# Input projections of a second block in three split products, its raw state parked in DRAM, and a last down group by token halves

## The chip, the cores and the metric

The kernel runs on one core of one Trainium2 chip. The metric is the device time of one execution in microseconds (us). Matrix products run on TensorE (PE in the profile), elementwise work on VectorE (DVE), ScalarE (ACT) and GpSimd (POOL), and SyncE (SP) issues most of the DMAs. The engines run their own instruction lists in order and wait for each other on semaphores.

## The reference, cut to what matters

Two transformer blocks follow each other on a state of 1024 tokens x 1024 features, in float32. The first has windowed attentions and a mixture of experts. Its output is `rms_norm(h, norm_final_g)`. The second block takes it as `x` and computes, in short:

```
hn   = rmsnorm(x) * attn_norm
proj = hn @ w_in_2             # q, k (256 each), v, gate (512 each), low (16), s5 u (256), rg x, rg gate (256 each)
y    = concat(gla(q, k, v, gate, low), s5(u), rg_lru(rx, rgate))
x    = x + y @ w_out_2
f    = rmsnorm(x) * mlp_norm
g, u = f @ w_up_2              # 2816 columns each
x    = x + (gelu(causal_conv(g)) * u) @ w_down_2
out  = rmsnorm(x) * final_norm
```

`gla` is a gated linear attention with four heads in chunks of 64 tokens; `s5` is a diagonal complex recurrence with 16 groups of 64 states; `rg_lru` is a gated real recurrence behind a short causal convolution.

## The kernel before

**Layout.** The state `hT` has features on partitions: eight tiles `Hp[k]` of 128 x 1024 (4096 KB in all). Work tiles are pages `Wp[i]` of the same size, and `Bp[k]` are eight of them. PSUM is used as four slots of 128 x 1024. `take()` numbers the uses of the slots in program order, and `slot(n)` waits until the use four earlier has been emptied. `mm_done` counts the products done.

**Weights.** SP loads weight units of 128 x 1024 into a ring of four places. Most products run as three: a float32 operand is split into a high part (fp32r, rounded) and the rest, and high x high, high x rest and rest x high are summed (`parts_tile`, L748 to 764: 48 matmuls of 512 columns for a 128 x 1024 output). For these GpSimd makes both parts of each weight unit (`split`, L554: a copy and a subtraction), in two buffers in turn. The 18 input units of the second block are the exception: they are used unsplit from the ring, in plain float32. `column_tile` (L708) gives 14 tiles of q, k, gate, u, rx and rgate with features on partitions; `token_tile` (L766) gives the four tiles of v with tokens on partitions, by swapping the operands. The first two columns run as `first_pair` (L718), tile by tile as the normalized state appears.

**Start of the second block.** The norm at the end of the first block and the one at the start of the second are folded: VectorE forms two rows of roots, spreads them on a diagonal (L1995), TensorE turns each into a full tile (L981), and VectorE writes `Bp[k]` (normalized input, L2001) and rescales `Hp[k]` in place (residual, L2005).

**S5 rounds.** For j = 0..8 TensorE's list is: the two state inputs of round j (L1025), one projection tile (L713), then the output product of round j-1 (L1044), which waits for GpSimd. In round 6 the low-rank product of 16 columns (L1033) stands behind the projection. VectorE multiplies the two state inputs from PSUM by a turning factor (L2078 to 2081), adds (L2083, L2084) and scans (L2085, L2086); GpSimd turns the states back with six operations on SBUF (L671 to 676) and asks for the factors two rounds ahead (L654). VR, VI and the factors have two buffers each.

**GLA.** Behind the rounds come three more value tiles, the gate products, norms, key transposes (L1073), chunk states (L1088), scores (L1098), and then the four heads: product of a head (L1123 to 1131), square on ScalarE, sum, root and scaling on VectorE, transposes (L1108). The output projection, whose first pair takes the parts that are ready first, follows.

**Feed-forward.** The 22 hidden tiles run in four groups of 6, 6, 6 and 4; behind each group the eight output tiles are updated by its product (`P_DOWN`, added into hT on L1817). With the last group VectorE also sums the squares for the final norm (L1528 after ScalarE's square, L1182). Then TensorE sums over partitions (L783), ScalarE takes roots, VectorE forms the diagonal (L1535), TensorE spreads it (L792), VectorE applies it tile by tile (L1546), and SP stores each tile.

## Time and profile before

| | us |
|---|---|
| three runs, median (lowest to highest) | 2489.38 (2489.29 to 2492.99) |
| the profiled execution, its own time | 2489.56 |
| its span in the trace | 2487.8 |
| TensorE busy | 2357.7 |
| GpSimd busy | 897.3 |
| VectorE busy | 1154.5 |
| ScalarE busy | 575.9 |

Times in the trace are counted from the start of the span. The second block starts at about 1216 us; its projections and S5 rounds run to about 1549, the four heads from 1601 to 1649. The granted clock of TensorE is given as a share of full speed: 1.00 is 2.4 GHz and 0.50 is 1.2 GHz. A float32 matmul appears as two records in the trace and overlaps its neighbours, so lengths of tiles are taken from start to start.

### The profile page before, as it was taken

To read this page: it belongs to the slowest core of one execution; us is meant where nothing else is said; L and a number is where in the kernel's file an instruction comes from. 1 tells how busy PE (TensorE), PEld (TensorE's weight loads), DVE (VectorE), ACT (ScalarE), POOL (GpSimd) and SP (SyncE) were. 2 spreads that over 40 slices of the span, in tenths; PEclk is the share of its full clock that TensorE was granted. 3 is DMA by queue.
4 is the path that set the end of the run, shared out by engine and by line. 5 is a ranking of instruction groups with operands and counts; after the bars stand their busy time and mean duration, and the time that the engine had idled before them with its cause. 6 is when DMAs were issued, how large, how long until landed. Compare 5 with 4: busy or idle time off the path is not lost.

```text
span 2487.8 us, 28689 instructions
## 1 busy us (share of the span) xinstructions
PE 2357.7 (95%) x11280; PEld 1799.0 (72%) x11280; DVE 1154.5 (46%) x1862; ACT 575.9 (23%) x809; POOL 897.3 (36%) x546
## 2 busy tenths in 40 slices
PE   7999999998999399998899999899999999999996
PEld 6888799997976266665444338778888888888885
DVE  7996444445522222222767856635432243133144
ACT  3100265676632111111121004111110011011011
POOL 2323534444423765700304861224332332332331
PEclk9999999999999799999899999779999999999998
DMA  4232122232322787822511210001111111111102
GB/s 153 77 119 85 50 67 75 67 90 69 114 94 95 285 303 298 311 102 110 190 40 45 76 59 26 9 27 50 49 40 47 60 41 45 60 49 39 58 26 76
DMA packets 76946, 228.76 MB, mean 92 GB/s; under 512 B 5456, under 2 KB 37328, under 8 KB 69904
## 3 DMA queue, kind: packets, MB, share of 16 engines
q1 hardware_dynamic: 58160, 140.60, 16.6%
q0 software_dynamic: 8576, 45.42, 5.0%
q10 hardware_dynamic: 10080, 40.90, 4.3%
q8 instruction: 94, 1.54, 0.3%
q14 instruction: 36, 0.29, 0.0%
HBM read 173.42 MB, written 53.48 MB: 91 GB/s over the span
## 4 chain that ended last, share of the span: by engine, by line
PE 91%; DVE 3%; issue 2%; ACT 1%; DMA 1%; POOL 1%; SPq 0%; DVEq 0%; POOLq 0%; ACTq 0%
PE ps L759 14%; PE ps L761 14%; PE ps L763 14%; PE ps L851 7%; PE ps L713 7%; PE ps L948 4%; PE ps L828 4%; PE ps L837 3%; PE ps L771 2%; PE ps L741 2%; PE ps L932 2%; PE ps L928 2%; PE ps L930 2%; PE ps L929 2%; PE ps L1025 1%
## 5 line engine op out<-in xcount | busy, mean ns | idle before, releaser
L759 PE MATMUL ps<-work_part 128*128 128x512 f32 x1568 | 484.0, 390 | 0.8 <-DVE work L2225 0.8
L763 PE MATMUL ps<-work_part 128*128 128x512 f32 x1568 | 482.7, 389 | 0.0
L564 POOL CAST work_part<-ring 128x1024 fp32r<-128x1024 f32 (+2 forms) x116 | 113.4, 977 | 825.1 <-PE ps L763 680.4
L761 PE MATMUL ps<-work_part 128*128 128x512 f32 x1216 | 374.4, 389 | 0.0
L759 PEld LDWEIGHTS ps<-work_part 128*128 128x128 f32 x1568 | 293.7, 188 | 62.2 <-DVE work L2225 1.3
L763 PEld LDWEIGHTS ps<-work_part 128*128 128x128 f32 x1568 | 294.4, 188 | 61.2
L568 POOL TENSOR_TENSOR work_part<-ring,work_part 128x1024 fp32r<-128x1024 f32 (+2 forms) x116 | 266.7, 2299 | 20.8 <-PE ps L1131 11.6
L761 PEld LDWEIGHTS ps<-work_part 128*128 128x128 f32 x1216 | 228.3, 188 | 47.4
L851 PE MATMUL ps<-work,hT 128*128 128x64 f32 x1600 | 195.8, 273 | 2.6 <-ACT hT L1251 2.1
L851 PEld LDWEIGHTS ps<-work,hT 128*128 128x128 f32 x1600 | 189.9, 193 | 4.6 <-ACT hT L1251 2.4
L1817 DVE TENSOR_TENSOR hT<-ps,hT 128x1024 f32<-128x1024 f32 x48 | 58.8, 1225 | 283.8 <-PE ps L763 267.3
L713 PE MATMUL ps<-work,ring 128*128 128x512 f32 x384 | 166.6, 592 | 0.0
L1768 DVE CUSTOM_DVE_ANT_0 hT<-ps,hT 128x1024 f32<-128x1024 f32 (+2 forms) x86 | 85.1, 990 | 130.1 <-PE ps L828 127.6
L713 PEld LDWEIGHTS ps<-work,ring 128*128 128x128 f32 x384 | 72.9, 190 | 91.4 <-issue 91.4
L828 PE MATMUL ps<-work_part 128*128 128x512 f32 (+1 forms) x448 | 125.5, 397 | 11.6 <-issue 8.1
L1499 ACT ACTIVATE work<-ps,cst 128x1024 f32<-128x1024 f32 x22 | 26.6, 1207 | 398.6 <-DVE ps L2220 398.6
L626 POOL TENSOR_TENSOR experts_lo<-pages,experts_hi 128x1024 fp32r<-128x1024 f32 x48 | 113.5, 2365 | 12.7 <-DMA pages<-w_moe 9.3
L948 PE MATMUL ps<-pages,work 128*128 x248 | 111.6, 592 | 1.6 <-DVE work L1949 1.6
L761 PE MATMUL ps<-hT_part,work_part 128*128 128x512 f32 x352 | 108.5, 390 | 0.0
L1242 ACT ACTIVATE hT<-hT,negm 128x1024 f32<-128x1024 f32 (+2 forms) x86 | 82.6, 961 | 97.1 <-DVE negm L1768 97.1
L1251 ACT ACTIVATE hT<-ps 128x1024 f32<-128x1024 f32 (+2 forms) x128 | 104.6, 818 | 1.4 <-PE ps L837 1.4
L2220 DVE TENSOR_TENSOR ps<-ps,cst 128x1024 f32<-128x1024 f32 x22 | 27.1, 1233 | 144.2 <-PE ps L763 137.6
(348 smaller groups left out, 3520.1 us busy)
## 6 DMA issues: line engine op xcount, KB each, us to landing
pages<-w_moe SPq DMA_DIRECT2D x16, 2048.0 KB, 9.2
ring<-w_up_units SPq DMA_DIRECT2D x44, 512.0 KB, 3.3
ring<-w_in_units SPq DMA_DIRECT2D x42, 512.0 KB, 3.5
pages<-w_moe SPq DMA_DIRECT2D x16, 1024.0 KB, 7.3
x_slots<-hT SPq DMA_DIRECT2D x31, 512.0 KB, 3.5
work<-x_slots ACTq DMA_DIRECT2D x31, 512.0 KB, 5.7
y_slots<-work ACTq DMA_DIRECT2D x31, 512.0 KB, 2.7
ring<-w_down_units SPq DMA_DIRECT2D x24, 384.0 KB, 3.0
```

Source lines behind the costliest of these rows:

```text
L564: pool.tensor_copy(WHI[n % 2][:, 0:cols], w).then_inc(whi_ready, 1)
L568: pool.tensor_tensor(WLO[n % 2][:, 0:cols], w, WHI_F[n % 2][:, 0:cols], ALU.subtract).then_inc(wlo_ready, 1)
L626: lo = pool.tensor_tensor(XLOW[:, at_lo:at_lo + S], w, hi.bitcast(f32), ALU.subtract)
L713: mm = pe.matmul(ps[:, half * HALF:(half + 1) * HALF], w[:, k * P:(k + 1) * P], rhs[k][:, half * HALF:(half + 1) * HALF], start=(k == 0), ...
L759: pe.matmul(ps[:, c], whi[:, w], hi[k][:, c], start=(k == 0), stop=False)
L761: pe.matmul(ps[:, c], whi[:, w], lo[k][:, c], start=False, stop=False)
L763: mm = pe.matmul(ps[:, c], wlo[:, w], hi[k][:, c], start=False, stop=(k == len(hi) - 1))
L828: mm = pe.matmul(ps[:, b * HALF:b * HALF + w], QS[h % 2][:, i * P:(i + 1) * P], part[h % 2][:, c0:c0 + w], start=(part is KH), stop=(part ...
L851: mm = pe.matmul(ps[:, 0:DH], PT[u % 2][:, j * P:(j + 1) * P], Wp[16 + k0 + j][:, h * DH:(h + 1) * DH], start=(j == 0), stop=(j == k1 - k0 ...
L948: mm = pe.matmul(ps[:, half * HALF:(half + 1) * HALF], HAT[b % 2][:, f * P:(f + 1) * P], xw[:, bass.ds(pages[b] + 4 * S + f * S + half * H ...
L1251: act.activation(PT[u % 2][:, 0:(k1 - k0) * P], PS[bank(n)][:, 0:(k1 - k0) * P], ACT.Copy).then_inc(pT_ready, 1)
L1768: dve.tensor_tensor_reduce(out=banks(SB[u % 3][:, 0:nk]), in0=scores, in1=banks(bias), scale=-1.0, scalar=3.0e38, op0=ALU.add, op1=ALU.min ...
```

## The change

- **Split projections.** The 18 input units of the second block run as `parts_tile`, too. The normalized input goes to three buffers `HN`; ScalarE rounds it to `HHI[k]` (in the pages of `Bp`) and VectorE writes the rest `HLO[k]` into the memory of hT. The ring's places 0 and 2 take the raw unit, ScalarE writes the high part into place 1 or 3 (`round_in2`), and GpSimd writes the rest over the raw unit (`rest_in2`), one unit ahead of each S5 round. A unit may be loaded when the product two units earlier is done.
- **Values.** The value tiles are computed with features on partitions, copied by ScalarE and turned by eight transposes (`turn_v`, `take_v`).
- **Low-rank product.** Its weights are split once by GpSimd; 48 matmuls of 512 columns take the place of 16 float32 ones.
- **State in DRAM.** Since HLO overwrites hT, SP stores hT to `h_keep` when the first block's last sum is in, VectorE waits for that after its first normalized tile, and SP loads it back behind the first four units of the output projection, after the fourth value transposes. The second root product (`spread_roots(1, P_FIRST)`) and the rescaling of hT (`residual`) move from the start of the stage into the heads.
- **Last down group.** It runs in two halves of the tokens: sixteen half tiles, each with its own split of the weight unit (loaded twice), half additions, and a final norm for each half. The first half's sums and root product stand behind half tiles 10 and 13; each result tile is stored in two halves.

```diff
@@ sync
+                if u == U_IN2 + 2:
+                    sp.wait_ge(ysum_ready, NT)
+                    sp.dma_start(h_keep, hT[:]).then_inc(h_moved, 16)
+                if u == U_OUT2 + RING:
+                    sp.dma_start(hT[:], h_keep).then_inc(h_moved, 16)
+                if U_IN2 + 2 <= u < U_OUT2:
+                    sp.wait_ge(mm_done, done(unit_use[u - 2]))
+                elif U_OUT2 <= u < U_OUT2 + RING:
+                    sp.wait_ge(mm_done, done(P_V2[3]))
@@ gpsimd
+            def rest_in2(n):
+                u = U_IN2 + n
+                hi, lo = wparts(u)
+                pool.wait_ge(whi_ready, u + 1)
+                pool.tensor_tensor(lo, ring[:, ring_at(u), :], hi.bitcast(f32), ALU.subtract).then_inc(wlo_ready, 1)
             for j in range(8):
                 vr, vi, ec, es = VR[j % 2], VI[j % 2], EC[j % 2], ES[j % 2]
+                rest_in2(7 + j)
                 pool.wait_ge(s5v_ready, j + 1)
...
+            for n in range(15, 18):
+                rest_in2(n)
@@ tensor
+            def half_tile(u, n, hi, lo, c, ready=None, base=0):
...
+                    pe.matmul(ps[:, c], whi[:, w], hi[k][:, c], start=(k == 0), stop=False)
+                    pe.matmul(ps[:, c], whi[:, w], lo[k][:, c], start=False, stop=False)
+                    mm = pe.matmul(ps[:, c], wlo[:, w], hi[k][:, c], start=False, stop=(k == len(hi) - 1))
@@ project
-                    if m < 14:
-                        column_tile(U_IN2 + m, MAIN[m], Bp)
-                    else:
-                        token_tile(U_IN2 + m, MAIN[m], Bp)
+                    parts_tile(U_IN2 + m, MAIN[m], HHI, HLO)
+            def turn_v(v):
+                pe.wait_ge(vt2_ready, v + 1)
+                ps = slot(P_V2[v])
+                for tt in range(NT):
+                    mm = pe.transpose(ps[:, tt * P:(tt + 1) * P], ring[:, 2 * (v % 2) + 1, tt * P:(tt + 1) * P], ident)
+                mm.then_inc(mm_done, 1)
-            first_pair(U_IN2, MAIN[0], MAIN[1], Bp, hn_ready, 0)
+            first_pair(U_IN2, MAIN[0], MAIN[1], HHI, xlo_ready, hn_lo0, HLO)
@@ heads
                 mm.then_inc(mm_done, 1)
+                if h == 0:
+                    spread_roots(1, P_FIRST)
@@ last down group
+                    for m in range(16):
+                        half_tile(u + m, P_LAST[m], hi, lo, FINAL[m // 8], ffact_ready if m == 0 else None, group[0])
+                        if m == 10:
+                            final_sum(0)
+                        if m == 13:
+                            final_root(0)
+            final_sum(1)
+            final_root(1)
@@ scalar
+            def round_in2(n):
+                u = U_IN2 + n
+                act.wait_ge(w_loaded[ring_at(u)], loads(u))
+                if n >= 2:
+                    act.wait_ge(mm_done, done(MAIN[n - 2]))
...
+                act.activation(wparts(u)[0], ring[:, ring_at(u), :], ACT.Copy).then_inc(whi_ready, 1)
                     m = main[0]
                     main[0] += 1
+                    if 1 <= m < 17:
+                        round_in2(m + 1)
                     act.wait_ge(mm_done, done(MAIN[m]))
@@ vector
+            for k in range(NT + 1):
+                if k < NT:
+                    if k >= 3:
+                        dve.wait_ge(xlo_ready, hn_lo0 + k - 2)
+                    dve.scalar_tensor_tensor(out=HN[k % 3], in0=Hp[k], scalar=both_gains[:, k:k + 1], in1=PS[bank(P_BOTH)][:, :],
+                                             op0=ALU.mult, op1=ALU.mult).then_inc(hn_ready, 1)
+                if k == 0:
+                    dve.wait_ge(h_moved, 16)
+                else:
+                    dve.wait_ge(hn_ready, k)
+                    dve.wait_ge(xhi_ready, hn_lo0 + k)
+                    dve.tensor_tensor(HLO[k - 1], HN[(k - 1) % 3], HHI[k - 1].bitcast(f32), ALU.subtract).then_inc(xlo_ready, 1)
...
             for h in range(4):
+                if h == 1:
+                    dve.wait_ge(roots_copied, 2)
+                    dve.wait_ge(h_moved, 32)
+                for k in ((), (0, 1, 2), (3, 4, 5), (6, 7))[h]:
+                    residual(k)
...
+            for m in range(16):
+                half, t = m // 8, m % 8
+                n, cols = P_LAST[m], FINAL[half]
+                dve.wait_ge(mm_done, done(n))
+                dve.tensor_tensor(Hp[t][:, cols], PS[bank(n)][:, cols], Hp[t][:, cols], ALU.add).then_inc(h_ready, 1)
+                if t >= 2:
+                    final_add(half, t - 1)
+                if m == 8:
+                    final_add(0, 7)
+                if m == 11:
+                    final_inverse(0)
+            final_add(1, 7)
+            for t in range(NT):
+                final_apply(0, t)
+            final_inverse(1)
+            for t in range(NT):
+                final_apply(1, t)
```

## Rows read from the trace of the kernel before

**Rows 1.** The page's part 4, the chain that ended last, shares by engine

```profile
PE 91%; DVE 3%; issue 2%; ACT 1%; DMA 1%; POOL 1%; SPq 0%; DVEq 0%; POOLq 0%; ACTq 0%
```

**Rows 2.** Windows: length, busy of PE, PEld, DVE, ACT, POOL, then granted clock, DMA

```profile
1326.00:1549.00 223.00, 223.00 (x812) 112.83 (x810) 170.66 (x93) 37.38 (x34) 127.55 (x54) 1.00 0.15 52
1601.00:1649.00 48.00, 48.00 (x217) 29.16 (x216) 20.64 (x36) 7.11 (x9) 10.78 (x7) 0.50 0.04 12
```

**Rows 3.** Timeline of TensorE: start, us, line and operation, records, idle before

```profile
1226.32 27.63 PE L741 MATMUL ps<-work,ring 128*128 128x512 f32 x64
...
1358.86 13.90 PE L713 MATMUL ps<-work,ring 128*128 128x512 f32 x32
1372.68 3.62 PE L1044 MATMUL ps<-work 128*32 128x512 f32 x8
1376.23 3.70 PE L1025 MATMUL ps<-work 128*128 128x512 f32 x8
...
1456.34 12.21 PE L1033 MATMUL ps<-work,cst 128*16 128x512 f32 x32
...
1494.74 14.56 PE L771 MATMUL ps<-ring,work 128*128 128x128 f32 x128
1509.23 3.62 PE L1044 MATMUL ps<-work 128*32 128x512 f32 x8
...
1569.68 16.16 PE L771 MATMUL ps<-ring,work 128*128 128x128 f32 x128 [1.91 <-DVE work L2158]
```

**Rows 4.** Timelines of VectorE and GpSimd in the S5 rounds

```profile
1383.43 1.22 DVE L2081 TENSOR_TENSOR work<-ps,work 128x1024 f32<-128x1024 f32 x1
...
1387.07 3.36 DVE L2084 TENSOR_TENSOR work<-work 128x1024 f32<-128x1024 f32 x1
...
1376.67 2.34 POOL L671 TENSOR_TENSOR work<-work 128x1024 f32<-128x1024 f32 x1 [3.54 <-DVE work L2086]
...
1397.05 2.34 POOL L671 TENSOR_TENSOR work<-work 128x1024 f32<-128x1024 f32 x1 [3.54 <-DVE work L2086]
...
1499.92 2.80 POOL L676 TENSOR_TENSOR work<-work 128x1024 f32<-128x1024 f32 x1
```

**Rows 5.** Timeline of VectorE in round 7, while GpSimd does nothing

```profile
1480.36 1.22 DVE L2083 TENSOR_TENSOR work<-work 128x1024 f32<-128x1024 f32 x1
...
1482.75 2.29 DVE L2085 TENSOR_TENSOR_SCAN work<-s5p,work 128x1024 f32<-128x1024 f32 x1
```

**Rows 6.** Timeline of VectorE and GpSimd in the last down group

```profile
2428.66 1.22 DVE L1817 TENSOR_TENSOR hT<-ps,hT 128x1024 f32<-128x1024 f32 x1 [4.22 <-PE ps L763]
...
2434.09 1.23 DVE L1817 TENSOR_TENSOR hT<-ps,hT 128x1024 f32<-128x1024 f32 x1 [4.21 <-PE ps L763]
...
2434.89 1.30 POOL L568 TENSOR_TENSOR work_part<-ring,work_part 128x512 fp32r<-128x512 f32 x1
...
2435.24 2.03 DVE L1528 TENSOR_TENSOR work<-work 128x1024 f32<-128x1024 f32 x1
```

**Rows 7.** Timeline of TensorE: the transposes of a head

```profile
1622.15 1.97 PE L1108 MATMUL ps<-cst,work 128*128 128x128 f32 x8
```

**Rows 8.** Start of the stage: timelines, the window 1218 to 1224, a DMA issue

```profile
1215.30 0.59 POOL L650 DMA_DIRECT2D work<-s_b  x1 [10.35 <-DVE hT L1978]
...
1224.60 9.62 DVE L2001 SCALAR_TENSOR_TENSOR work<-hT,small,ps 128x1024 f32<-128x1024 f32 x8 [2.44 <-PE ps L981]
...
1218.00:1224.00 6.00, 3.54 (x13) 0.79 0.98 386
...
hT<-xT POOLq DMA_DIRECT2D x1, 4096.0 KB, 14.2
```

**Rows 9.** Window of TensorE behind its wait of 1.91: busy, granted clock

```profile
1570.00:1572.00 2.00, 2.00 (x11) 0.50 0.00 0
```

**Rows 10.** The end: the last root product, and the window behind it

```profile
2470.53 3.78 PE L792 MATMUL ps<-work,cst 128*128 128x512 f32 x4 [1.85 <-DVE work L1535]
...
2474.00:2476.00 2.00, 0.31 (x1) 0.95 0.00 0
```

More of the change, by code:

```diff
@@ L201, in build, with in2, ring_at, loads @@
         U_UP = U_OUT2 + 8
-        split_units = list(range(0, U_IN2)) + list(range(U_OUT2, len(units)))
+        split_units = list(range(len(units)))
         split_of = {u: n for n, u in enumerate(split_units)}
+        def in2(u):
+            return U_IN2 <= u < U_OUT2
+        def ring_at(u):
+            return 2 * ((u - U_IN2) % 2) if in2(u) else u % RING
+        def loads(u):
+            return 16 * sum(ring_at(v) == ring_at(u) for v in range(u + 1))
+        def wparts(u):
+            if in2(u):
+                return Wr[37 + ring_at(u) + 1][:, :], Wr[37 + ring_at(u)][:, :]
+            return WHI[u % 2], WLO[u % 2]
         at = [0]
@@ L320, in build @@
         P_TTURN = take(1)
-        P_BOTH, P_FIRST = take(1), take(1)
+        P_BOTH = take(1)
+        hn_lo0 = split_base[0]
+        split_base[0] += NT
+        HN = [Wp[6], Wp[7], Wp[8]]
+        HHI, HLO = [Wr[29 + k][:, :] for k in range(NT)], [hTr[k][:, :] for k in range(NT)]
+        P_V2 = []
         MAIN = [take(1) for _ in range(3)]
@@ L355, in build @@
             {"o": P_O, "turn": P_OT}[what][h] = take(1)
+            if (what, h) == ("o", 0):
+                P_FIRST = take(1)
         OSQ, ON = [Bp[4], Bp[5]], [Wp[21], Wp[22]]
@@ L410, in build @@
         for m in range(18):
-            emptied[MAIN[m]] = (in2_ready, m + 1)
+            emptied[MAIN[m]] = (in2_ready, m + 1) if m < 14 else (vt2_ready, m - 13)
+        for v in range(4):
+            emptied[P_V2[v]] = (in2_ready, 14 + v + 1)
         for m in range(2):
@@ L429, in build @@
         for what, i in FFN_STEPS:
-            unit_use += [P_UP[i], P_UP[i] + 1] if what == "up" else [P_DOWN[i] + m for m in range(8)]
+            unit_use += [P_UP[i], P_UP[i] + 1] if what == "up" else P_LAST if i == 3 else [P_DOWN[i] + m for m in range(8)]
         Mp = Wp[25:29]
@@ L723, in first_pair @@
                 else:
-                    ws = [(WHI[split_of[u + i] % 2], WLO[split_of[u + i] % 2]) for i in range(2)]
+                    ws = [wparts(u + i) for i in range(2)]
                 last = len(hi) - 1
@@ L1993, in _, with roots_diag @@
             link(dve.reciprocal(troots, troots))
-            for i in range(2):
+            def roots_diag(i):
                 dve.tensor_tensor(TDIAG[i].rearrange("p (t n) -> p t n", n=P),
```

228 lines of the change are left out of this document (166 added, 62 removed).

## The prediction

> **What bounds the kernel now.** I read the chain that ended last first: TensorE stands for 91% of it [rows 1]. Then the stretches of the second block. From 1326 to 1549 us TensorE is busy in every one of the 223 us at the full clock (1.00, 2.4 GHz), VectorE for 171 and GpSimd for 128 of them; from 1601 to 1649 us it is just as busy, but at half clock (0.50, 1.2 GHz) [rows 2]. So in the projections and the S5 rounds TensorE's own time sets the pace. Less of it saves time only until the next thing is late, so the question is what is late next. For that I read one S5 round on TensorE [rows 3], the same round on VectorE and GpSimd [rows 4], and the same operations where the other engine was silent [rows 5].
>
> **What the change is worth on TensorE.** A plain column tile takes 13.82 us (1358.86 to 1372.68), a value tile 14.5 us at full clock [rows 3]. A tile of 24 split matmuls takes 5.43 us (2428.66 to 2434.09), 0.227 us each [rows 6], so one of 48 takes 10.9. Fourteen column tiles save 2.95 each, 41 us. A value tile adds eight transposes, 1.97 us at half clock [rows 7], 1.0 at full, and saves 2.6: 10 us for four. The low-rank product goes from 12.2 us [rows 3] to 48 x 0.227 = 10.9, 1 us. That is 52 us if TensorE stayed the bound, and a floor of about 2437. I do not think it stays the bound in any of the stages.
>
> **Start of the stage.** Before, the normalized tiles start at 1224.60 and the first pair runs from 1226.32 to 1253.95 [rows 3, 8]. Now the first low part overwrites a tile of hT, so VectorE waits, after one tile, until all 4096 KB of hT are in DRAM, with all its later work queued behind. The store can start when the last sum into hT is done, at 1215. Bounds: the load of the same size took 14.2 us [rows 8], so 1229 if it has the DMA engines to itself. But GpSimd's queue issues 3328 KB of loads from 1215.30 on: together 7.6 MB, at the 386 GB/s of 1218 to 1224 us [rows 8] 19.7 us, plus 1 to 2 us to land: 1236 to 1237. I take 1236, since these loads are certainly there. Then each tile costs VectorE two operations of 1.2 us [rows 8], 2.4 us. Low part 0 is ready at 1238.6, 3 at 1245.8, 7 at 1254. TensorE goes tile by four: the third product of tile 3 at 1247, four of the second column 5.4, four of the first 5.4, four of the second 5.4: 1263.3, 9.4 us later than before. The third tile's weights may only be loaded when the first is done (1257.9): load 3.6, rounding on ScalarE 1.2, rest on GpSimd 2.5, so it starts at 1265.5, 11.7 us late. Four tiles follow before the S5 rounds, 4 x 2.95 = 11.8 back. The clock costs 2, since TensorE sits idle from 1223 to 1238, and a wait of 1.91 was enough for 0.50 behind it, at the cost of 16.16 instead of 14.5 [rows 3, 9]. The rounds start 2 us later than before (bounds -5 by the store alone, +5 if its share is smaller).
>
> **The S5 rounds.** TensorE's round is 3.5 + 3.5 + 13.8 = 20.9 us and would be 18.0. But VectorE and GpSimd hold each other up. Alone, VectorE's sum takes 1.22 and its scan 2.29 [rows 5]; beside GpSimd the same sum takes 3.36 [rows 4], as if it waited for the 2.34 of one GpSimd operation. VectorE's products that read PSUM stay at 1.22 [rows 4]. So operations with two SBUF inputs on the two engines take turns. Per round: GpSimd 6 x 2.34 = 14.0, VectorE 2 x 1.14 + 2 x 2.2 = 6.7, together 20.7 (GpSimd's rounds start 20.38 apart, 1376.67 to 1397.05, with some overlap at the ends). The cover of this was TensorE's 20.92: the pair is at its limit already. Now each round gives GpSimd one more such operation, the rest of a weight unit: 2.3 us. That this form takes turns too is seen at the half size: VectorE's sum beside it took 2.03 instead of 1.22, and ended 1.08 after it did (2436.19 to 2437.27) [rows 6]. So a round takes 20.4 + 2.3 = 22.7 us, against 20.9: **slower, not faster**. Bounds for the rest's cost per round: 0 if it falls where VectorE reads PSUM, 4.6 if it also delays GpSimd's start by a turn; I take 2.3 by the row.
> The Trainium skill (*SBUF — State Buffer*, section "SBUF: two separate sides") says that the pair of ports shared by the two is an exclusive lock held for the whole instruction, also for a VectorE operation with two SBUF inputs against a GpSimd one that reads SBUF. The trace agrees (3.36 against 1.22). If the two engines only shared a bandwidth, the extra operation would cost a part of its 2.3 us, and the round would stay nearer to 20.4.
> Over the rounds: the end of GpSimd's eighth was 1502.7 (1499.92 + 2.80) [rows 4], hidden behind TensorE, whose last S5 output product ended at 1512.85 [rows 3]. Seven rounds behind the first cost 1.8 each, 12.6; the one with the low-rank product stays TensorE's and gets 1.3 shorter; and the 6.5 us which a value tile had put between GpSimd's end and the last product (1502.7 to 1509.23) are used up: +5, so that product ends at 1519.9, 7 us later than before. TensorE waits some 4 us per round for it, so the clock falls in some of them (a wait of 1.91 did it [rows 3, 9]); most of that is hidden in the wait, the last is not: the product at half clock, +2 (bounds 0 and 15).
>
> **Between the rounds and the heads.** The rounding for the next weight unit stands on ScalarE behind the wait for that last product: 1.2 + 2.5 and up to 2.3 of turns, 5 us of idle TensorE. Two tiles give 3.6 each, two transposes take 1 each, and VectorE's and ScalarE's chain behind the gate products goes on as before: 0 to +4, I take +2. The third transpose, at half clock, stands ahead of the key transposes: +1.5. The fourth value tile (16.16 us [rows 3]) was what VectorE waited for, 9 us: 10.9 plus 1.6 of half clock, -3.7. So the heads start 2 + 5 + 2 + 2 + 1.5 - 3.7 = 9 us late.
>
> **The heads.** The second root product now stands here, behind head 0. Its like, the last root product, took 3.78 us at half clock [rows 10]: +3.7. Its copy, the eight rescaled tiles of hT (1.2 each, two or three a head) and the reload of 4096 KB (asked for some 8 us before head 0, landed some 10 us into it) lie beside heads of 12.5 us on TensorE (three transposes of 1.97 taken from the 48 us of [rows 2] leave 10.5 for one of four heads). VectorE's own per head, at 1.2 an operation of this size, is three rescalings, a reduction, a scaling, a gate, a wait for ScalarE's rounding, a rest and 1.7 for the root: 10.3. Cost 0; if heads ran at full clock they would be the bound.
>
> **The last down group.** Sixteen half tiles of 12 matmuls take the same 43.5 us. Each asks GpSimd for a split within 2.72 us. Before, from the sum at 2434.09 to the end of the rest at 2436.19 it was 2.1 us, with 0.35 of signals [rows 6]: 2.45. VectorE's half addition of squares now gets in ahead of the rest: +0.4, so 2.85, 0.14 late, 2 us over fourteen. Sums and root of the first half take 1.8. So the last tile ends at 2465 instead of 2461.1 (five tiles of 5.43 behind 2434.09, less the 0.15 of a signal). Behind it was 26.7 us: addition, square, addition, sums, roots, the root product of 3.78, eight applications of 9.62 [rows 10, 8] and the last store. Now 2.5 to the sums, 1.4 for sums and roots; VectorE's eight half applications of the first half (4.9) lie across this; then the diagonal 0.9, half a root product 1.9, eight half applications 4.9, store 3.2, in all 18.5. So -8.2 + 3.8 = **-4.4** (bounds -6.5 and -2).
>
> **Sum.** 9 + 3.7 - 4.4 = +8.3. The profiled execution took 2489.56 (span 2487.8 and 1.8 around it), the median of the runs 2489.38, so the one stands for the other: 2498.
>
> **Rivals.** (A) *The root product brings the clock back.* From 1601 to 1649 us TensorE is busy all the time at half clock, and the three transposes of 1.97 us did not raise it [rows 2, 7]. Bursts of full-size products did: behind the root product of 2470.53, 3.78 us, the next 2 us were granted 0.95; the value tile of 1569.68 lost only 1.7 us in all, so it was back in some 3.4 [rows 3, 10]. The added root product is such a burst. If the clock rises behind it, the three heads left take 5.3 instead of 10.5 and VectorE (10.3 a head) becomes their bound. The last head is normalized at 10.5 + 3 + 3 x 10 = 43 us from the start of head 0 instead of 51 (48 + 3) before, and the first output pair ends 16 us behind it (its transposes 1, 11 of 16 tile steps of 1.36), at 59 instead of 72: 13 us earlier than before instead of 3.7 later, 2498 - 16.5 = 2481.5. For: the bursts. Against: it is the shortest of them, between products of 64 rows and columns. This is the case on the faster side: it decides itself in the 4 us after the added product. (B) *The rest finds free turns*: rounds stay at 20.4, 7 x 2.3 = 16 less, but then the value tile is again between, which keeps 3: 2485. Against: 20.4 of 20.4 us are taken. (C) *The clock falls in every round and stays down into the projections*: 7 rounds of 2 us more: 2512. For: waits of 4 us. Against: 48 full-size products in each round. (D) TensorE stays the bound throughout, as if nothing waited: 2489.6 - 52 + 3.7 - 4.4 = 2437. Against: rows 4.
>
> **Chances.** Forecast 0.45; A 0.35; B 0.10; C 0.07; D 0.03. A measurement of this kernel tells 0.2%, 5 us, from no change: the limits are 2484.4 and 2494.4. Of the forecast's 0.45, with +-5 around 2498, 0.33 lies above 2494.4 and the rest within; of A, 0.27 is faster and 0.07 within; B gives 0.06 faster and 0.03 within, C is slower, D faster. With 0.36, 0.21 and 0.43. The range leaves out D, the far end of A and of C: 2478 to 2506; the forecast's own is 2492 to 2504.
>
> **What would show it.** GpSimd's rounds starting 22 to 24 us apart (20.4 would be B, 18 D); VectorE's first low part at 1238 and the first pair's end near 1263; TensorE waiting 3 to 5 us before each S5 output product; the granted clock of the heads, 0.50 (forecast) or 1.00 behind the added root product (A); 18 to 19 us from the last down tile to the end. I am wrong if the rounds come at TensorE's pace, or if the heads take 40 us instead of 52.

## The result and the profile after

The changed kernel takes 2477.26 us (median of 5 runs, 2474.35 to 2478.99) beside 2489.38 of the kernel before (5 runs, 2483.72 to 2492.99): a ratio of 0.9943, 95% interval 0.9931 to 0.9956. It is 0.6% faster, where the forecast said 0.35% slower. The time is just below the forecast's range, and within 5 us of what rival A gave. The profile is of the fastest of the five executions (2474.35).

Part 4 of the page after, the chain that ended last (the view of [rows 1]), and the two long windows of [rows 2], now of the changed kernel:

```profile
PE 83%; DVE 6%; POOL 5%; issue 3%; DMA 2%; ACT 2%; SPq 0%; DVEq 0%; POOLq 0%; ACTq 0%
```

```profile
1326.00:1549.00 223.00, 194.78 (x688) 119.27 (x687) 187.31 (x90) 49.00 (x45) 163.31 (x64) 0.93 0.15 52
1601.00:1649.00 48.00, 43.61 (x272) 28.75 (x272) 38.04 (x48) 10.46 (x13) 10.90 (x7) 0.93 0.22 89
```

TensorE's share fell from 91% to 83%: in the projections and rounds it now works 195 of 223 us, and GpSimd 163 instead of 128. The second row is where the gain is: the heads' stretch, at 0.50 before, is at 0.93.

For the ledger I read the same marks in both timelines: the last sum into hT (1213.8 before, 1214.3 after), the end of the first pair (1254.0, 1256.9), the first state input of the rounds (1317.3, 1311.5), the end of the last S5 output product (1512.8, 1512.2), the start of head 0 (1600.8, 1599.8), the end of the first output pair (1673.1, 1659.6), the last down tile (2461.2, 2454.1) and the end.

| stretch, us | before | after | measured | forecast |
|---|---|---|---|---|
| ahead of the last sum into hT | 1213.8 | 1214.3 | +0.5 | 0 |
| sum to first pair's end | 40.2 | 42.6 | +2.4 | +9.4 |
| to the rounds | 63.4 | 54.5 | -8.9 | -7.4 |
| rounds, to the last output product | 195.5 | 200.8 | +5.3 | +5 |
| to head 0 | 88.0 | 87.6 | -0.4 | +2 |
| head 0 to first output pair's end | 72.3 | 59.8 | -12.5 | +3.7 |
| to the last down tile | 788.2 | 794.5 | +6.3 | +3.8 |
| behind it | 26.6 | 18.4 | -8.2 | -8.2 |
| sum | | | -15.5 | +8.3 |

(The sum is of rounded marks; the spans differ by 15.3.)

The stretch "to the rounds" took 54.5 us here and 56.2 in most other profiles with the split tiles. The difference is the clock. Behind the first pair TensorE waits 2.3 us for the rest of the next weight unit in all of them; in this execution the clock stays at 1.00 behind the wait, in the one of experiment 2 it falls for some 3 us. So the same wait can go either way (first row: the changed kernel, second row: experiment 2, each 2 us behind that wait):

```profile
1258.92:1260.92 2.00, 1.72 (x8) 1.47 (x9) 1.96 (x2) 0.79 (x1) 0.13 (x1) 1.00 0.29 117
1267.12:1269.12 2.00, 2.00 (x6) 1.57 (x5) 2.00 (x2) 0.32 (x1) 1.61 (x1) 0.50 0.00 0
```

**Start.** The timeline of VectorE, and DMA issues of the window 1215 to 1234 with the packets of the two queues:

```profile
1225.10 1.28 DVE L2175 SCALAR_TENSOR_TENSOR work<-hT,small,ps 128x1024 f32<-128x1024 f32 x1 [3.57 <-PE ps L1079]
1229.46 1.28 DVE L2175 SCALAR_TENSOR_TENSOR work<-hT,small,ps 128x1024 f32<-128x1024 f32 x1 [3.08 <-DMA h_keep<-hT]
1230.66 1.22 DVE L2182 TENSOR_TENSOR hT_part<-work,work_part 128x1024 fp32r<-128x1024 f32 x1
```

```profile
q1 hardware_dynamic: 144, 4.19, 57.2%
q0 software_dynamic: 440, 2.95, 36.9%
...
h_keep<-hT SPq DMA_DIRECT2D x1, 4096.0 KB, 13.9
...
work<-s_b POOLq DMA_DIRECT2D x1, 1024.0 KB, 14.6
```

The wait is there, but 3.1 us long, not 10: the store landed in 13.9 us, as if alone (a load of the same size took 14.2 [rows 8]), and it was GpSimd's loads that took longer: 14.6 us for the first, which took 5.0 in the kernel before.

**Rounds.** GpSimd and VectorE in the rounds, as in [rows 4], then TensorE's product behind them:

```profile
1398.12 2.41 POOL L737 TENSOR_TENSOR work<-work 128x1024 f32<-128x1024 f32 x1 [4.41 <-DVE work L2262]
...
1411.95 4.32 POOL L742 TENSOR_TENSOR work<-work 128x1024 f32<-128x1024 f32 x1
...
1417.16 3.40 POOL L714 TENSOR_TENSOR work_part<-ring,work_part 128x1024 fp32r<-128x1024 f32 x1
1420.53 2.34 POOL L737 TENSOR_TENSOR work<-work 128x1024 f32<-128x1024 f32 x1
```

```profile
1414.06 4.36 DVE L2262 TENSOR_TENSOR_SCAN work<-s5p,work 128x1024 f32<-128x1024 f32 x1
```

```profile
1416.33 4.95 PE L1153 MATMUL ps<-work 128*32 128x512 f32 x8 [7.32 <-POOL work L742]
```

The rounds start 22.4 us apart here (1398.12 to 1420.53). From the first start to the eighth (1326.80 to 1489.09) it is 23.2 on the mean: the first round took 25.9, the one with the low-rank product 23.3, the others 22.4 to 23.0. The rows show the turns: VectorE's scan, 2.29 alone [rows 5], begins at 1414.06 but takes 4.36, since GpSimd's last operation of the round (L742) runs to 1416.27. The rest (L714) begins at 1417.16, within the scan, and ends at 1420.56, 2.1 us behind the scan's end. TensorE waits up to 7.3 us for GpSimd ahead of its output product.

**Heads.** Windows (length, busy of PE, PEld, DVE, ACT, POOL, granted clock, DMA) and TensorE's timeline:

```profile
1600.00:1606.00 6.00, 6.00 (x48) 3.66 (x45) 5.59 (x17) 0.00 (x0) 4.89 (x3) 1.00 1.01 434
1606.00:1609.00 3.00, 0.12 (x4) 0.00 (x0) 2.86 (x6) 1.02 (x1) 0.00 (x0) 0.63 0.84 360
1609.00:1613.00 4.00, 3.84 (x6) 1.30 (x8) 2.66 (x4) 0.32 (x2) 0.00 (x0) 0.50 0.00 0
1613.00:1636.00 23.00, 22.33 (x169) 14.36 (x170) 16.86 (x15) 5.02 (x7) 6.54 (x4) 0.99 0.08 24
```

```profile
1597.03 2.00 PE L1200 MATMUL ps<-work 64*128 64x256 f32 x16 [1.64 <-DVE work L2350]
...
1609.16 3.78 PE L1079 MATMUL ps<-work,cst 128*128 128x512 f32 x4 [3.04 <-DVE work L2160]
```

Head 0 already runs at 1.00. Then TensorE waits 3.04 us for VectorE's diagonal, the clock falls, the added root product takes 3.78 us at half speed, and behind it the clock is back for the other three heads. That part is rival A as it was written; that head 0 is fast too was in no case. Nearly all of what head 0 gains goes into the wait: the diagonal is done at 1609.1, and a head 0 of 10.5 us would have ended at 1610.3, behind it. After that VectorE sets the pace of the heads, as A had it: its reductions for the four heads start at 1609.02, 1620.55, 1631.43 and 1640.32.

**End.** TensorE in the first half tile, and VectorE's last operation:

```profile
2408.01 0.50 PE L843 MATMUL ps<-work_part 128*128 128x512 f32 x1 [1.77 <-DVE work_part L2417]
```

```profile
2464.49 5.36 DVE L2442 SCALAR_TENSOR_TENSOR hT<-hT,cst,ps 128x512 f32<-128x512 f32 x8 [2.17 <-PE ps L862]
```

### The profile page after: what moved, and what is told of

Its sections match the earlier page's. It is cut to its first block, busy times and chain, and to the rows that moved or that the text cites. A ratio compares the mean times of both kernels' runs of the same rounds, so it can differ in the third digit from the quotient of the medians.

```text
span 2472.5 us, 28776 instructions
## 1 busy us (share of the span) xinstructions
PE 2304.1 (93%) x11232; PEld 1816.8 (73%) x11232; DVE 1192.5 (48%) x1895; ACT 609.4 (25%) x849; POOL 976.6 (39%) x582
## 4 chain that ended last, share of the span: by engine, by line
PE 83%; DVE 6%; POOL 5%; issue 3%; DMA 2%; ACT 2%; SPq 0%; DVEq 0%; POOLq 0%; ACTq 0%
PE ps L827 15%; PE ps L829 15%; PE ps L831 15%; PE ps L949 7%; PE ps L926 4%; PE ps L1046 4%; PE ps L935 3%; PE ps L1030 2%; PE ps L1026 2%; PE ps L1028 2%; PE ps L1027 2%; PE ps L809 1%; PE ps L811 1%; PE ps L812 1%; PE ps L1014 1%
## 5 line engine op out<-in xcount | busy, mean ns | idle before, releaser
L827 PE MATMUL ps<-work_part 128*128 128x512 f32 x1760 | 548.9, 393 | 8.5 <-POOL work_part L714 6.0
L831 PE MATMUL ps<-work_part 128*128 128x512 f32 x1760 | 543.2, 390 | 0.0
L613 POOL CAST work_part<-ring 128x1024 fp32r<-128x1024 f32 (+2 forms) x124 | 118.5, 956 | 808.9 <-PE ps L831 659.7
L827 PEld LDWEIGHTS ps<-work_part 128*128 128x128 f32 x1760 | 330.4, 188 | 83.4 <-issue 12.6
L831 PEld LDWEIGHTS ps<-work_part 128*128 128x128 f32 x1760 | 331.3, 188 | 69.5
L829 PE MATMUL ps<-work_part 128*128 128x512 f32 x1152 | 354.6, 389 | 0.0
L617 POOL TENSOR_TENSOR work_part<-ring,work_part 128x1024 fp32r<-128x1024 f32 (+2 forms) x124 | 281.0, 2266 | 15.9 <-PE ps L1244 6.1
L829 PEld LDWEIGHTS ps<-work_part 128*128 128x128 f32 x1152 | 216.2, 188 | 44.9
L829 PE MATMUL ps<-hT_part,work_part 128*128 128x512 f32 x608 | 189.2, 393 | 0.0
L1982 DVE TENSOR_TENSOR hT<-ps,hT 128x1024 f32<-128x1024 f32 x40 | 49.0, 1225 | 261.5 <-PE ps L831 244.9
L829 PEld LDWEIGHTS ps<-hT_part,work_part 128*128 128x128 f32 x608 | 115.1, 189 | 24.3
L1656 ACT ACTIVATE work<-ps,cst 128x1024 f32<-128x1024 f32 x22 | 26.6, 1208 | 398.3 <-DVE ps L2404 398.3
L637 POOL CAST work_part<-work 64x1024 fp32r<-64x1024 f32 x16 | 16.5, 1031 | 204.6 <-PE ps L926 196.3
L714 POOL TENSOR_TENSOR work_part<-ring,work_part 128x1024 fp32r<-128x1024 f32 x18 | 51.0, 2836 | 116.5 <-ACT work_part L1497 116.4
```

The source lines that it names most:

```text
L613: pool.tensor_copy(WHI[n % 2][:, 0:cols], w).then_inc(whi_ready, 1)
L617: pool.tensor_tensor(WLO[n % 2][:, 0:cols], w, WHI_F[n % 2][:, 0:cols], ALU.subtract).then_inc(wlo_ready, 1)
L827: pe.matmul(ps[:, c], whi[:, w], hi[k][:, c], start=(k == 0), stop=False)
L829: pe.matmul(ps[:, c], whi[:, w], lo[k][:, c], start=False, stop=False)
L831: mm = pe.matmul(ps[:, c], wlo[:, w], hi[k][:, c], start=False, stop=(k == len(hi) - 1))
```

## The experiments

Runs of all kernels differ by several us ahead of the point where the change begins (the last sum into hT ends its wait between 1213.8 and 1220.5 in the profiled executions), so each kernel is also read by its stretches. Most stretches that an edit leaves alone repeat within 1 us, but the first one differs by up to 3 us (38.6 to 41.5 among kernels with the old start), and a wait behind which the clock falls only in some executions adds 1.7 us to "to the rounds" or 1.6 to the feed-forward part ("FFN" in the table). All are in the table behind the last experiment. The number behind each time is its ratio to the kernel before as run beside it (medians from 2490.16 to 2493.95), with its 95% interval; where times of different kernels are compared, the ratios count.

**1. A burst behind head 0, in the kernel before.**

```diff
+                if h == 0:
+                    ps = slot(P_BURST)
+                    for half in range(2):
+                        mm = pe.matmul(ps[:, half * HALF:(half + 1) * HALF], ones, Hp[0][:, half * HALF:(half + 1) * HALF],
+                                       start=True, stop=True)
+                    mm.then_inc(mm_done, 1)
```

> The kernel before with one more product behind head 0: the same shape as the root product of the changed kernel (four records of 128x512, read from tile 0 of hT, its result used by nobody). Theory 1 (a product of this size brings the clock back, small head products do not): the product takes 3.8 us at half clock, then heads 1 to 3 run at 1.00, 6.3 instead of 10.6 us each and their transposes 1.05 instead of 1.97: 3.8 - 3 x 5.2 = -12 us, about 2477. Theory 2 (the clock of the heads in the changed kernel has another cause): the heads stay at 0.50 and it is 3.8 us slower, 2493.

2479.88 us, ratio 0.995 (0.9931 to 0.9968). Windows before and behind the burst, and the burst:

```profile
1605.00:1618.00 13.00, 12.27 (x56) 7.17 (x56) 9.97 (x29) 0.00 (x0) 7.59 (x5) 0.50 0.00 0
1622.00:1643.00 21.00, 21.00 (x163) 13.67 (x164) 10.72 (x11) 5.40 (x7) 5.16 (x4) 1.00 0.08 27
```

```profile
1618.31 3.31 PE L1140 MATMUL ps<-hT,cst 128*128 128x512 f32 x4
```

A product that nobody uses makes the kernel before 13.8 us shorter in its stretch (72.3 to 58.5). Theory 1 holds.

**2. The changed kernel with a short root product.** The roots spread over 896 of the 1024 tokens are left out.

```diff
+                if i == 1:
+                    pe.matmul(ps[:, 0:P], ones, TDIAG[i][:, 0:P], start=True, stop=True).then_inc(mm_done, 1)
+                    return
```

> The changed kernel with its second root product cut to one product of 128x128 (the rescaling of hT then uses wrong roots: that part of the computation is left out). The 3 us wait in front of it stays. Theory 1 (the full product brought the clock back): the clock falls in the wait and heads 1 to 3 run at 0.50, +4.3 us a head and +0.9 a transpose, less 3.3 for the product, +12 us, about 2489. Theory 2 (the clock comes back by itself after a short wait): 3 us faster, 2474.

2489.53 us, 0.9992 (0.998 to 1.0004): the whole gain is gone.

```profile
1602.00:1613.00 11.00, 8.54 (x68) 5.50 (x66) 10.40 (x33) 5.43 (x7) 10.20 (x7) 1.00 1.06 447
1618.00:1653.00 35.00, 35.00 (x158) 21.21 (x156) 21.12 (x20) 5.72 (x8) 4.43 (x3) 0.50 0.05 16
```

```profile
1616.63 0.79 PE L1079 MATMUL ps<-work,cst 128*128 128x128 f32 x2 [3.04 <-DVE work L2163]
```

The same wait lowers the clock; 35 us of TensorE busy all the time with head products do not bring it back. The two experiments show both directions: with the long product of 512 columns behind the wait heads 1 to 3 are fast, without it they are not.

**3. The rests of the rounds left out** (third products of units 7 to 14 take the rounded weights).

```diff
+                c = slice(0, 8) if 7 <= n < 15 else slice(0, S)
-                pool.tensor_tensor(lo, ring[:, ring_at(u), :], hi.bitcast(f32), ALU.subtract).then_inc(wlo_ready, 1)
+                pool.tensor_tensor(lo[:, c], ring[:, ring_at(u), c], hi[:, c].bitcast(f32), ALU.subtract).then_inc(wlo_ready, 1)
```

> The changed kernel with GpSimd's rest of the weight units 7 to 14, those of the S5 rounds, cut to 8 of 1024 columns (their third product takes the rounded weights instead: that part of the computation is left out, TensorE's work is the same). Theory 1 (the rounds are set by the operations of GpSimd and VectorE taking turns): GpSimd's rounds start 20.4 apart instead of 22.7, seven rounds of 2.3: 16 us faster, about 2461. Rival (TensorE's chain of waits sets the rounds): 22.7 apart and no change. Second rival (TensorE's own 18 us a round would be the bound as soon as the rest is gone): 33 us faster, 2444.

2468.75 us, 0.9909 (0.989 to 0.9928): 8.5 us less than the changed kernel, where 16 was expected.

```profile
1396.16 2.35 POOL L738 TENSOR_TENSOR work<-work 128x1024 f32<-128x1024 f32 x1 [5.67 <-DVE work L2265]
...
1416.72 2.35 POOL L738 TENSOR_TENSOR work<-work 128x1024 f32<-128x1024 f32 x1 [2.26 <-DVE work L2265]
```

20.6 us apart, where it was 20.4 before the change [rows 4]; the rounds take 187.2 instead of 200.8. So one rest costs a round some 2 us, about what it takes, though TensorE's own work is the same. Of the 13.6 us 6 are given back on the way to head 0 (93.6 instead of 87.6), where ScalarE's and VectorE's chain for the gates then ends last: TensorE waits 4.9 us for it ahead of the sums (2.7 in the changed kernel).

**4. The end alone, in the kernel before** (the diff's last down group, nothing else).

> The kernel before with the last down group by token halves alone. By the two traces (last tile 6.2 us later, what follows it 8.2 shorter): 2.0 us faster, 2487. By the forecast's terms (3.8 and 8.2): 4.4 us faster, 2485. If the half tiles cost more beside other data: no change or slower.

2488.23 us, 0.9988 (0.9973 to 1.0003). By its stretches 792.9 and 18.4 instead of 788.2 and 26.6: -3.5 us, which the runs alone cannot tell from nothing. Within the half tiles there is one long wait, 1.77 us for the last activation, as in the changed kernel.

**5. Three waits, two of them filled, in the kernel before.**

```diff
-                    for j in range(4):
+                    for j in 2 * [0, 1, 2, 3] if m == 1 and q4 in (1, 2) else range(4):
```

> The kernel before, with two of its chunk products (the ones in front of the waits of 1.34 and 1.65 us just ahead of head 0) computed twice, 1 us each, so that the waits become some 0.3 and 0.6 us; no burst behind head 0. Theory 1 (the clock falls in these short waits, and what the heads lack is only something that brings it back): it does not fall, head 0 and all after it run at 1.00, from 46.5 to 27 or 28 us, and the product that ran at half speed gains 1: 19 to 20 us faster, about 2472. Rival (the heads' own small products lower the clock, whatever stands before them): it falls within head 0 and nothing is gained, 2491.

2493.1 us, 1.001 (0.9996 to 1.0024): nothing gained.

```profile
1598.00:1603.00 5.00, 3.75 (x30) 2.40 (x26) 4.75 (x19) 0.00 (x0) 4.92 (x3) 1.00 0.00 0
1605.00:1651.00 46.00, 46.00 (x208) 27.39 (x206) 20.04 (x34) 6.09 (x8) 9.22 (x6) 0.50 0.04 12
```

```profile
1604.74 0.69 PE L1123 MATMUL ps<-work 128*64 128x128 f32 x4 [1.68 <-DVE work L2158]
```

The edit did only half of what its expectation said. The clock now held through the two filled waits, but the third, 0.73 us before, had grown to 1.68, and there it fell. That left two readings: the wait, or the heads.

**6. All three filled.** The same line with `q4 in (1, 2, 3)`.

> The kernel before with its last three chunk products computed twice (the two of the run before, and the last one too): there the clock had still fallen, but only in the wait of 1.7 us between the last chunk product and head 0. Now that wait is some 0.7. Theory 1 (the clock falls where TensorE waits, and no product of the heads lowers it): it holds, the heads take 27 to 28 us instead of 46.5: 19 us faster, 2472. Rival (the heads' small products lower it by themselves): it falls in head 0 or 1, under 4 us gained.

2470.31 us, 0.9919 (0.9905 to 0.9933). From 72.3 to 50.8 us for the stretch.

```profile
1595.00:1602.00 7.00, 5.43 (x45) 3.93 (x41) 6.63 (x25) 0.30 (x2) 6.81 (x5) 1.00 0.00 0
1603.00:1630.00 27.00, 27.00 (x209) 17.28 (x210) 19.82 (x34) 6.54 (x9) 9.54 (x7) 1.00 0.07 21
```

```profile
1602.51 0.44 PE L1123 MATMUL ps<-work 128*64 128x128 f32 x4 [0.81 <-DVE work L2158]
```

Three products computed twice make the kernel before 20 us faster, more than the whole change does (0.9943). Here the heads' products do not lower the clock; in experiments 2 and 5 they fail to raise it. The edit shortens the waits and puts more work between them at the same time; the two were not separated.

**7. The changed kernel's transposes alone, in the kernel before.** What kept head 0 fast in the changed kernel was open; beside the sizes of the tiles, the order ahead of it had changed by the fourth value tile's transposes.

```diff
+            ps = slot(P_TURNS)
+            for tt in range(NT):
+                mm = pe.transpose(ps[:, tt * P:(tt + 1) * P], Hp[0][:, tt * P:(tt + 1) * P], ident)
+            mm.then_inc(mm_done, 1)
             chunk_states(1)
```

> The kernel before with eight transposes (of tile 0 of hT, the result used by nobody) between the scores and the last four chunk products, where the changed kernel has the transposes of its fourth value tile. Theory 1 (this part of the change is what kept the clock at 1.00 through head 0: the products there then come in pairs behind the waits, as in the changed kernel): it costs 1.1 us or nothing, and the heads take 27 to 28 us instead of 46.5: 18 to 19 us faster, 2473. Rival (the clock in the changed kernel held for another reason, such as the three products in place of the value tile): it falls ahead of head 0 as before, 0 to 1 us slower, 2492.

2469.99 us, 0.9906 (0.9883 to 0.9929). The time is as expected, the way is not:

```profile
1594.00:1599.00 5.00, 4.03 (x38) 3.30 (x37) 4.66 (x18) 3.30 (x4) 2.98 (x2) 1.00 0.01 3
1602.00:1605.00 3.00, 3.00 (x16) 2.07 (x14) 2.80 (x9) 0.00 (x0) 2.92 (x3) 0.50 0.00 0
1606.00:1632.00 26.00, 26.00 (x202) 16.61 (x202) 18.18 (x31) 6.10 (x8) 8.22 (x6) 1.00 0.07 21
```

```profile
1598.93 1.13 PE L1090 MATMUL ps<-work 64*128 64x256 f32 x8 [0.97 <-DVE work L2180]
1601.71 3.54 PE L1090 MATMUL ps<-work 64*128 64x256 f32 x16 [1.65 <-DVE work L2180]
1605.18 0.54 PE L1129 MATMUL ps<-work 128*64 128x128 f32 x4
```

The clock did fall behind the wait of 1.65, and two chunk products in a row, 3.54 us at half speed, brought it back before head 0. One more use of a PSUM slot moves each chunk product by one slot, so that the last two wait together and then run without a gap. In the changed kernel they come in twos as well (x16, 2.00 us), and there the clock did not fall at all. So this part of the change is enough for a fast head 0, by a clock that comes back. That it is also why the clock did not fall in the changed kernel is not shown.

**8. The store on GpSimd's queue**, behind its loads, in the changed kernel.

```diff
-                    sp.dma_start(h_keep, hT[:]).then_inc(h_moved, 16)
+            load_turns(1)
+            pool.wait_ge(ysum_ready, NT)
+            pool.dma_start(h_keep, hT[:]).then_inc(h_kept, 16)
```

> The changed kernel with the store of hT issued by GpSimd, on its own queue and behind its loads, instead of by SyncE. Theory 1 (the store had landed in 13.9 us because SyncE's queue is served before GpSimd's loads): now it shares or follows, lands at 19 to 21 us, and VectorE's first low part, TensorE's first pair and all behind them come 6 to 7 us later, 2484. Rival (the order of issue decides nothing and the loads were slow for another reason): it lands in 14 us again, no change.

2485.04 us, 0.9976 (0.9966 to 0.9987).

```profile
h_keep<-hT POOLq DMA_DIRECT2D x1, 4096.0 KB, 19.7
work<-s_turns POOLq DMA_DIRECT2D x2, 1024.0 KB, 9.0
work<-s_b POOLq DMA_DIRECT2D x1, 1024.0 KB, 5.2
```

19.7 us, which is the forecast's number for both transfers together, and the first pair ends 51.0 us behind the last sum: +10.8 against the kernel before, where the forecast had +9.4. The forecast was right on one queue and wrong on two. On two, q1 moved 4.19 MB in 144 packets, 29 KB each, and q0 2.95 MB in 440, 6.7 KB each. The Trainium skill (*DMA: Bandwidth & Descriptors*, section "Queues, rings and completion order") says that a DMA engine goes round its queues and changes after a whole packet. The trace agrees as far as it goes. My estimate by that rule: served in turn by whole packets, the store gets 4.3 times the bytes of the loads, which is 81% of the 386 GB/s [rows 8], and 4.19 MB take 13.4 us (measured 13.9). The first load, 1024 KB, landed at 1230.4, 1.0 us behind the store; at 386 GB/s it would have needed 2.7 if it had begun only then, so it moved beside the store. The run changed the queue and the order of issue together, so it shows that the queue or the order matters and not which; that the share goes by the size of the packets is argued.

**9. The root product behind head 1, the rescaling of hT behind the last head**, in the changed kernel.

```diff
-                if h == 0:
+                if h == 1:
                     spread_roots(1, P_FIRST)
-                for k in ((), (0, 1, 2), (3, 4, 5), (6, 7))[h]:
-                    residual(k)
...
+                    if parts and m + 3 < NT:
+                        residual(m + 3)
```

> The changed kernel with the second root product behind head 1 instead of head 0, and the eight rescalings of hT on VectorE behind the last head instead of between the heads. Theory 1: the wait of 3.0 us and the fall of the clock behind it (2.6 us more for the product) go, and VectorE's chain no longer sets the last heads: from head 0 to the end of the first output pair 4 to 6 us less, 2472. Rival (the pair's end is set by the last head's low part on VectorE and by what is behind it): 1 us or less.

2472.09 us, 0.9918 (0.9902 to 0.9935); the stretch is 52.5 instead of 59.8, 7 us and not 4 to 6. The product now takes 1.98 us at full clock, and TensorE hardly waits from head 0 on:

```profile
1605.00:1634.00 29.00, 28.84 (x213) 17.97 (x214) 21.18 (x37) 7.33 (x12) 9.64 (x6) 1.00 0.36 146
```

**10. Four edits together:** number 9, the store in four pieces, the rounding of unit 15 ahead of the wait for the last output product, and the first two half tiles by turns.

```diff
+                    for k in range(NPIECE):
+                        c = slice(k * NT // NPIECE, (k + 1) * NT // NPIECE)
+                        sp.dma_start(h_keep[:, c, :], hT[:, c, :]).then_inc(x_loaded[k], 16)
+            round_in2(15)
             act.wait_ge(s5x_ready, 8)
+                for ks in (range(3), range(3, 4)):
+                    for i in range(2):
```

> The changed kernel with four edits, to be told apart by stages: the store of hT in four pieces, each low part waiting for its own (first low part at once, first pair 3 us earlier); the rounding of weight unit 15 ahead of the wait for the last S5 output product (3.7 us of TensorE's wait go, unless VectorE's gating chain is then the bound, as it was with shorter rounds: 0); the root product behind head 1 (4 to 6 us); the first two half tiles of the last down group computed by turns, three parts each and then the fourth (the wait of 1.8 us and 2 us of half clock go: 3.8). Together 11 to 16 us faster than the changed kernel, 2462 to 2467. If the stages only pass the waits on: under 6.

2471.1 us, 0.9922 (0.9899 to 0.9945), over a wide range (2463.85 to 2481.73): 6 us less in the median than the changed kernel, not 11 to 16. The pieces gave their 2.6 us (40.0 instead of 42.6). The rounding and the half tiles by turns gave next to nothing: TensorE's wait of 3.71 us for unit 15 went, but one of 1.60 for the next unit came, and its wait ahead of the sums grew from 2.67 to 4.96; the wait for the last activation gave way to one of 1.56 for the third split. In this execution the clock fell 2.7 us into head 0, with TensorE busy since its start, and the root product brought it back:

```profile
1599.00:1601.00 2.00, 2.00 (x17) 1.22 (x15) 1.86 (x6) 0.00 (x0) 2.00 (x2) 1.00 1.02 442
1602.00:1618.00 16.00, 16.00 (x74) 9.28 (x72) 8.25 (x17) 1.32 (x2) 1.80 (x1) 0.50 0.31 132
```

**11 and 12. Store in pieces and number 9, without and with the chunk products computed twice.** The diffs are those of 10 and 6.

> The changed kernel with the store in four pieces and the root product behind head 1 with the rescalings behind the heads. Theory 1: first pair 2.7 us earlier behind the last sum into hT, from head 0 to the end of the first output pair 52.6 us if the clock holds (one earlier profile) and 61.5 if it falls in head 0 (another one): 2467 or 2475. Rival: the clock always holds without the 3 us wait: 2467 and a narrow spread.

> The same with the last three chunk products computed twice, which fills the waits ahead of head 0 to under 1 us each. Theory 1 (the waits lower the clock): it always holds, 52.6 us for that stretch, 2467. Rival (they don't, the fall in head 0 comes from elsewhere): as the run without the filling, or 1 to 3 us slower by the added products.

2469.4 us, 0.9906 (0.9892 to 0.9919), and 2469.9 us, 0.9909 (0.9895 to 0.9923). Both held the clock (52.4 and 52.5 us). The filling showed nothing here: two profiles of three without it (9, 10 and 11) held anyway, so the fall in head 0 of number 10 is not settled by it.

**13. Only the clock and the end, in the kernel before:** numbers 4 and 6.

> The kernel before with its last three chunk products computed twice and the last down group by token halves, and nothing else of the change: 20.8 us from the heads (stretch of head 0 to the end of the first output pair, 50.8 instead of 71.3 us) and 3.4 from the end (half tiles 4.8 longer, what follows 8.2 shorter). 24 us faster, 2467; the heads alone gave 2470. Rival (the half tiles give nothing): 2470.

2468.87 us, 0.9915 (0.9888 to 0.9941). The lowest median, but not to be told from 2469.4 to 2470.3 of numbers 6, 7, 11 and 12. It splits no projection and parks nothing. One of its six executions took 2484.79 us, 16 more than the median. It was not profiled, so whether the clock fell in it is open.

| us | sum to pair | to rounds | rounds | to head 0 | heads, pair | FFN | tail |
|---|---|---|---|---|---|---|---|
| before | 40.2 | 63.4 | 195.5 | 88.0 | 72.3 | 788.2 | 26.6 |
| after | 42.6 | 54.5 | 200.8 | 87.6 | 59.8 | 794.5 | 18.4 |
| 1 burst | 40.1 | 63.4 | 195.5 | 88.1 | 58.5 | 788.1 | 26.6 |
| 2 short product | 42.6 | 56.2 | 200.5 | 87.4 | 72.2 | 792.9 | 18.4 |
| 3 no rests | 42.6 | 56.2 | 187.2 | 93.6 | 59.8 | 794.6 | 18.4 |
| 4 end alone | 40.2 | 63.4 | 195.5 | 88.1 | 72.6 | 792.9 | 18.4 |
| 5 two filled | 38.6 | 63.4 | 195.5 | 87.8 | 72.3 | 788.1 | 26.5 |
| 6 three filled | 38.6 | 63.4 | 195.5 | 88.1 | 50.8 | 788.2 | 26.5 |
| 7 transposes | 40.0 | 63.4 | 195.5 | 90.0 | 50.8 | 788.1 | 26.1 |
| 8 other queue | 51.0 | 56.2 | 200.7 | 87.8 | 59.8 | 792.9 | 18.3 |
| 9 root behind head 1 | 42.6 | 56.1 | 200.4 | 87.4 | 52.5 | 794.5 | 18.3 |
| 10 four edits | 40.0 | 54.6 | 200.1 | 87.8 | 61.3 | 793.2 | 18.3 |
| 11 pieces and 9 | 39.5 | 56.2 | 200.3 | 87.4 | 52.4 | 794.6 | 18.4 |
| 12 the same, filled | 39.3 | 56.2 | 200.5 | 88.3 | 52.5 | 793.0 | 18.3 |
| 13 clock and end | 41.5 | 63.4 | 195.5 | 88.1 | 50.8 | 792.9 | 18.4 |

## Why the prediction was wrong

It was wrong by 21 us in the median and 24 in the profiled execution, and nearly all of it lies in two steps.

**The heads (16 of the 24 us): the wrong case was chosen.** "Its like, the last root product, took 3.78 us at half clock: +3.7" was right as far as it went: 3.78 is what it took. The step failed in taking half clock for the heads behind it. Rival A had the mechanism and its size (59 us for the stretch, measured 59.8), and experiments 1 and 2 show it both ways. That A's size came out so well is partly luck: head 0 took 6 us instead of its 10.5, and the wait of 3.04 us ahead of the product, which it did not have, took most of that back. I weighed against it that the product stands between products of 64 rows and columns. The rows for it were in the rival's own paragraph: behind 3.78 us of 512-column product the clock was back [rows 10], behind 1.97 us of transposes and 48 us of head products it was not [rows 2, 7]. There was evidence on which product raises the clock and none on what its neighbours do; 0.35 gave it too little weight. The forecast also took head 0's half clock as given, because the kernel before had it. In experiments 5 to 7 the clock ahead of head 0 changed with the waits and with what ran between them, and each edit ahead of the heads shifts those.

**The start (7 us): a term mis-sized.** "I take 1236, since these loads are certainly there" adds the bytes of two queues and divides by one rate, as if the store ended last. The lower bound of the same paragraph, 1229, is what came (1229.46). On one queue, behind the loads, the sum was exact (experiment 8).

**The rounds were right**, in place and cause, and in size on the whole: +5.3 for +5, most rounds 22.4 to 23.0 us (forecast 22.7), and without the rests 20.6 (experiment 3). Only the first round, 25.9 us, was longer than the sum had it. VectorE's operation with two SBUF inputs waits for GpSimd's and the other way round; this is also where most of TensorE's 52 us went. Since the stage began 7 us earlier than forecast, the last product ended where it had before.

**To head 0** the cost of 5 us at unit 15 was 3.7, and the chain behind it took up what the shorter tiles gave: -0.4 for +2. **The end**: the tail was exact (18.4 for 18.5), the half tiles cost 6.3 for 3.8. In place of GpSimd's splits it was the first half tile, which reaches its last part 2 us sooner than a full tile and so waits 1.77 us for the activation. In some executions the clock dips behind this (1.6 us more in this one and in experiments 3, 9 and 11: 794.5 beside 792.9 in others with the same wait).

**Slips in the sums** that decided nothing: low part 7 is ready at 1255.4 by its own terms, not at 1254, and the parts named for the chances add up to 0.36, 0.22 and 0.40.

**What the change is worth.** The clock of the heads gave 12.5 of its 15.5 us, as a side effect, and 21.5 were to be had without it. All the rest of the change together gave 3. The 21.5 is the stretch of experiment 6, whose edit also gives head 0.

**Open**: why the clock fell within head 0 in experiment 10 and not in 9 and 11, nor in the changed kernel and experiments 2, 3 and 8, whose waits ahead of head 0 are the same (1.16, 1.65 and 0.8 us). Its end part by turns and its rounding lie elsewhere. The waits of 2.3 and 1.77 us named above go either way in the same sense, so a wait of given length makes a fall of the clock possible here, not certain. Another place for the rests of the rounds was not tried.

## What to carry to other kernels

Before an edit is priced at TensorE's two speeds, list the waits ahead of each long stretch of small products, and ask which product behind them could raise the clock: here three chunk products computed twice gave 20 us and one product that nobody used 14 in its stretch, while 52 us of TensorE's work saved gave 3 with all that it cost. Look at more than one execution, since the same wait lowers the clock in some and not in others. Where GpSimd and VectorE are in turns all the time, work moved to GpSimd costs about its whole length. Transfers on two queues are not one sum: here the store of 4096 KB took 13.9 us and the loads beside it paid, and in one queue behind them it took 19.7.

## What the runs showed of the hardware

- Products that bring the granted clock back to 1.00 after waits: the root product of 3.78 us (512 columns), the burst of 3.31, two chunk products in a row, 3.54 (256 columns). Products that do not: 0.79 us of one short root product, a chunk product of 2.08 with a wait behind it, and 35 to 46 us of head products (64 to 128 columns, many on 64 rows) without a gap. The Trainium skill (*TensorE: Matmul & The Clock Gate*, section "What's actually happening") says that the clock is set by how busy TensorE has been recently. By the busy share of the trace that does not fit here: in experiments 2 and 5 TensorE is busy in all of 35 and 46 us and the clock stays at 0.50.
- At full clock the head products mostly keep it: 27 us at 1.00 in experiment 6. In experiment 10 it fell 2.7 us into them, without a wait.
- Waits of 0.47, 0.79 and 0.81 us with products of 2 us between them left the clock up (experiments 6 and 13); 1.34, 1.65 and 0.73 with products of 1.1 to 2.1 between lowered it, in all three profiles of that order (before, 1, 4). 1.16, 1.65 and 0.8 with products of 2.0 between left it up in six profiles of seven. One wait of 2.3 us, and one of 1.77, lowered it in some profiles and not in others.
- GpSimd's subtraction of 8 columns in experiment 3 took 0.2 us at the least and 1.25 where it began within one of VectorE's scans (1413.20 to 1414.45, the end of the scan): in these rows it waits for its turn, however small it is.
